# Attention on one core: the value products moved into fewer, longer runs between turns and scores

## The reference, cut to what matters

```
for blk in range(S // Q_BLOCK):                       # 16 blocks of 128 queries
    s = einsum("bhqd,bhkd->bhqk", q[block], k[:q1])   # scores against all earlier keys
    s = s + cum[q] - cum[k]                           # forget gates
    p = softmax(where(causal, s, -inf))
    outs.append(einsum("bhqk,bhkd->bhqd", p, v[:q1])) # value products
```

## Time and profile before

| | |
|---|---|
| median of 3 runs | 2429.84 us (2429.21 to 2431.21) |
| the profiled execution's own time | 2430.31 us |
| its span, first to last instruction | 2428.5 us |
| TensorE clock granted, mean | 0.995 |
| PE busy | 2377.7 us, 98% |
| DVE busy | 1355.0 us, 56% |
| ACT busy | 1121.2 us, 46% |
| the attention in the span | about 704 to 1534 us |

### The profile page before, as it was taken

One profiled execution on the slowest core, in us unless ns is written; L12 is line 12 of the kernel. 1 busy time (PEld: TensorE's weight loads), 2 busy tenths in 40 slices (PEclk: granted clock), 3 DMA queues, 4 the chain that ended last, 5 costly groups with the idle time before them and its releaser, 6 DMA issues. The chain is left out here.

```text
span 2428.5 us, 36529 instructions
## 1 busy us (share of the span) xinstructions
PE 2377.7 (98%) x13441; PEld 2046.7 (84%) x13441; DVE 1355.0 (56%) x2766; ACT 1121.2 (46%) x2036; POOL 616.3 (25%) x717
## 2 busy tenths in 40 slices
PE   8999999999999999999999999989999999999998
PEld 7888889999887888888888888877888888887787
DVE  4232112111014888888888888836544566667633
ACT  2131111101115888888888888832014465657300
POOL 0000000000001455554555554525430000000343
PEclk9999999999999999999999999999999999999999
DMA  6525444232126454566544566266533453447672
GB/s 200 141 75 140 114 121 122 105 122 104 65 90 150 98 117 110 119 138 136 119 117 110 121 137 138 89 204 207 180 122 98 141 160 126 136 136 248 222 256 82
DMA packets 221258, 328.78 MB, mean 135 GB/s; under 512 B 17420, under 2 KB 144716, under 8 KB 215260
## 3 DMA queue, kind: packets, MB, share of 16 engines
q1 hardware_dynamic: 220568, 325.91, 47.2%
q0 software_dynamic: 512, 0.53, 0.1%
HBM read 199.89 MB, written 126.48 MB: 134 GB/s over the span
## 5 line engine op out<-in xcount | busy, mean ns | idle before, releaser
L926 DVE TENSOR_TENSOR at_pl<-at_tps,at_ph 128x512 fp32r<-128x512 f32 (+3 forms) x640 | 371.1, 605 | 16.0 <-ACT at_ph L849 16.0
L849 ACT ACTIVATE at_ph<-at_tps 128x512 fp32r<-128x512 f32 (+3 forms) x640 | 319.1, 537 | 125.7 <-PE at_tps L763 117.7
L324 ACT ACTIVATE pa_stg<-pa_ps 128x512 fp32r<-128x512 f32 (+1 forms) x128 | 76.5, 598 | 635.9 <-PE pa_ps L252 635.9
L763 PE MATMUL at_tps<-ident,at_probs 128*128 128x128 f32 x2176 | 340.6, 274 | 8.5 <-DVE at_pl L926 7.2
L783 PE MATMUL at_ops<-at_ph,at_val 128*128 128x256 f32 (+1 forms) x1152 | 315.5, 296 | 0.2 <-DVE at_pl L926 0.2
L839 ACT ACTIVATE at_probs<-at_probs,at_least 128x128 f32<-128x128 f32 (+15 forms) x256 | 308.0, 1203 | 0.1
L252 PE MATMUL pa_ps<-pa_xh,pa_wh 128*128 128x512 f32 x768 | 300.3, 391 | 3.4 <-DVE pa_wl L377 3.4
L252 PE MATMUL pa_ps<-pa_xh,pa_wl 128*128 128x512 f32 x768 | 299.4, 390 | 0.0
L252 PE MATMUL pa_ps<-pa_xl,pa_wh 128*128 128x512 f32 x768 | 299.3, 390 | 0.0
L783 PE MATMUL at_ops<-at_pl,at_val 128*128 128x256 f32 (+1 forms) x1152 | 294.9, 282 | 0.0
L749 PE MATMUL at_sps<-at_k,at_q 128*128 128x512 f32 (+3 forms) x640 | 277.8, 434 | 10.3 <-DVE at_probs L918 7.8
(11 more groups left out here) (184 smaller groups left out, 4624.8 us busy)
## 6 DMA issues: line engine op xcount, KB each, us to landing
at_q<-q_halves SPq DMA_DIRECT2D x45, 512.0 KB
at_k<-k_halves SPq DMA_DIRECT2D x45, 512.0 KB
q_halves<-pa_stg SPq DMA_DIRECT2D x32, 512.0 KB, 3.8
k_halves<-pa_stg SPq DMA_DIRECT2D x32, 512.0 KB, 3.7
v_halves<-pa_stg SPq DMA_DIRECT2D x32, 512.0 KB, 2.8
y_gated<-re_work SPq DMA_DIRECT2D x32, 512.0 KB, 3.1
at_val<-v_halves SPq DMA_DIRECT2D x15, 1024.0 KB, 17.3
pa_wst<-in_attn_w_in SPq DMA_DIRECT2D x14, 1024.0 KB, 7.1
```

What stands on the lines that cost most here:

```text
L324: nc.scalar.activation(out, source(kind, s), func, scale=scale).then_inc(evac_h, 1)
L763: mm = nc.tensor.transpose(tps[c % TB][:, k, :], probs[s % ROWS][:, t0:t0 + P], ident[:, :])
L849: nc.scalar.activation(ph[g % 2][:, j * PB:j * PB + n, i % 2 * P:(i % 2 + 1) * P], tps[c % TB][:, 0:n, :], ACT.Copy).then_inc(high_out, 1)
L926: nc.vector.tensor_tensor(pl[g % 2][at], tps[c % TB][:, 0:n, :], raw(ph[g % 2][at]), ALU.subtract)\
```

## The change: where value products stand in a step

The change is in `step` of the tensor program. It makes a list `slots` of the places behind which value products may stand: the parts that have a turn next, and the last part. Of these it keeps every second one, counted so that the last stays in; it drops those ahead of j = 3, but keeps the last one if nothing is left. The step's value products are then divided evenly over the slots. How many key tiles a step multiplies, and every other engine's program, stay as they are.

```diff
                 order = alternate(scores_now, turns, -1)
+                slots = [j for j in range(parts) if j + 1 == parts or order[j + 1][0]]
+                slots = slots[(len(slots) + 1) % 2::2]
+                slots = [j for j in slots if j >= SKIP] or slots[-1:]
                 for j in range(parts):
                     if order and order[j][0]:
                         turn(t_it, t_s, order[j][1])
                     elif order:
                         score(it, s, order[j][1])
-                    if weighing:
-                        k0, k1_ = (lo + (hi - lo) * max(j + d - SKIP, 0) // max(parts - SKIP, 1) for d in range(2))
-                        if j + 1 == parts:
-                            k1_ = hi
+                    if weighing and j in slots:
+                        k0, k1_ = (lo + (hi - lo) * (slots.index(j) + d) // len(slots) for d in range(2))
                         if k1_ > k0:
                             weigh(w_it, w_g, k0, k1_)
```

## The result

The changed kernel takes 2440.61 us (median of 6 runs, 2438.09 to 2442.19) against 2430.68 for the kernel before on the same chips: a ratio of 1.0039, 95% interval 1.003 to 1.0049, or 9.9 us more. The forecast was slower, 2447 us, with a range of 2430 to 2456. The sign and the mechanism were right; 9.9 us were measured of the 17 that the sum gave. Of all executions in this study one, the profiled one of the kernel with less work in block 1, took 5990 us and is left out.

A forecast was written before the change was run, and what follows sets the result against it. PE was taken to bound blocks 0 to 4, DVE blocks 8 to 15. Lateness behind last scores and in block 15 summed to 1.11 us a head, 17 us taken on 2430: 2447 us, range 2430 to 2456.

The forecast's parts named there:

- the sum: Lateness after blocks 9 and 11 to 14, and in block 15: 1.11 us a head, 17.8 us over 16 heads, taken as 17.
- the mechanism: Blocks 8 to 14: products behind a step's last score, which a take pins, delay the next block's second score, by 0.02 to 0.28.
- What bounds blocks 8 to 15: DVE takes and subtracts back to back (24.37 of 25.13 us busy in blocks 8 to 14); PE, though seemingly busy, waits.
- the signs that were named: DVE waits at second takes and block 15's third; blocks 8 to 14 grow 0.7 to 0.8 us, block 15 some 0.35.
- the term for the arrival: From PE's end of a score to the take waiting for it: 0.29 us, used in every line from block 9 to 15.
- The extra time of a score that has waited: A score that waited runs slower: 0.57 us full, 0.28 for 128 columns, 0.38 and 0.47 interpolated for 256 and 384.
- the lower end: If a score that waited cost no more than any other, the sum would be 0.66 us a head, 11 us.
- Late by 0.35, if the second score came just in time: Block 15, second to third take: PE needs 1.63 us with three key tiles ahead of the third turn, DVE 1.28.
- The cost of 0: Blocks 0 to 2: products move behind the fourth turn, PE's sum decides and stays the same; neither cost nor gain.
- Hidden: Rival: DVE's few tenths in hand absorb PE's lateness in blocks 9 to 15; within 0.2%, 2430 to 2435; chance 0.17.
- Faster: Rival: PE bounds throughout, and scores following turns at once remove half its 33 us of waits: 2414 us; chance 0.08.
- Much slower: Rival: DVE has nothing in hand, every key tile moved in blocks 8 to 15 counts whole: 65 us, 2495; chance 0.05.

The follow-up runs named there:

- blocks 12 to 14 alone: New rule for product portions in blocks 12, 13 and 14 only, old rule elsewhere, against the kernel before: 2438.93 us, ratio 1.0038.
- the kernel with the early fourth turn: Kernel before, but in block 15 no products ahead of the fourth turn, two key tiles behind it, four at the end: 2429.58 us, ratio 0.9998.
- the combined kernel: Kernel before with block 15's fourth turn early, half of block 0's products ahead of its third turn, blocks 0 to 2's rest behind the fourth: 2426.51 us, 0.9983.

## Why the prediction was right, and what its sum got wrong

*What bounds blocks 8 to 15.* Right. VectorE is back to back there, PE waits, and taking 0.48 us of PE's work out of blocks 9, 11 and 13 gained nothing in any of them.

*The mechanism.* Right, and shown from two sides. The last score of a step is pinned by a take; what stands behind it delays the next block's scores. The same run ahead of that score costs nothing (ratio 1.0006), behind it 8 us (1.0038 with blocks 12 to 14 alone). For a run of 4 or 5 key tiles it is the place and not the length as such. Of the signs that were named, PE's waits moved from a first score to the last ones, and blocks 0 to 4 kept their time; but blocks 8 to 14 grew by 0.36 us and not by 0.7 to 0.8, and the takes that came late were the first ones, and not the second.

*The size.* The step that was off is the term for the arrival, "from PE's end of a score to a take that waits for it ... 0.29 us", as applied to second takes. It was read at a first take. After the change, first takes start 0.30 us behind their score's end (1260.00 to 1260.30), but second takes at most 0.21 (1260.91 to 1261.12), without waiting, and the third take of block 15, which does wait, 0.20. With the first takes as the ones that come late, the prediction's own terms give 0.08 at block 9, 0.09 at 12 (0.82 + 0.28 + 0.94 + 0.91 + 0.29 = 3.24 against 1253.43 - 1250.28 = 3.15), 0.18 at 13, 0 at 14, and with an arrival of 0.20 in block 15, 0.26. That is 0.61 us a head, where 0.61 was measured (0.04, 0.11, 0.15, 0.01, 0.29, and 0.01 here and there). That the two are equal is in part luck: the single blocks are off by up to 0.04 both ways, and the 0.20 is read from the very take whose delay it is to give. The extra time of a score that has waited, for which the lower end was worked out, was right: 0.27 to 0.28 us for 128 columns in the new trace too (1257.85 to 1258.12). So the 9.9 us lie near the lower end of 11, but not for that end's reason. The rule of the Trainium skill that was weighed there (TensorE: Matmul & The Clock Gate, What happens when you issue a matmul: weight loads are pulled ahead of matmuls in flight) does not help a score that waits: in the new trace it is again the weight load that is held, 88 times for 43.9 us, and the matmul behind it for 8.1 us.

*Block 15.* "Late by 0.35, if the second score came just in time" was the right form: alone it costs 0.00, behind blocks 12 to 14 it costs 0.29. What I had not seen is that the lead, once lost, is paid in any case: with the old order in block 15 it came out in blocks 0 to 3, so that the loss belongs to blocks 12 to 14. Of these, block 14's run takes the lead away even where block 13's is shorter.

*Blocks 0 to 2.* The cost of 0 was right, for a wrong reason. "PE is busy all the time" there, "PE's sum decides": it does not. PE's modelled ends cover its waits: the stretch shows 15.97 us busy of 15.97, with a wait of 0.62 us in front of block 0's third turn and the 0.36 in front of block 3's first product in it. Leaving work out of block 1 gained little or nothing and filling the wait of block 0 nothing, and only block 3 gave its 0.48 us back. The chain of waits as the runs show it: from block 15's fourth turn over ScalarE to the lows of block 2, for which the first product of block 3 waits. In the kernel before, ScalarE goes without a break from 1212.37, where it waited for that turn, to the lows' inputs of block 2:

```profile
1212.37 0.28 ACT L849 ACTIVATE at_ph<-at_tps 128x128 fp32r<-128x128 f32 x1 [0.45 <-PE at_tps L763]
1212.55 1.90 ACT L839 ACTIVATE at_probs<-at_probs,at_least 128x1920 f32<-128x1920 f32 x1
...
1215.23 1.85 ACT L849 ACTIVATE at_ph<-at_tps 128x512 fp32r<-128x512 f32 x4
1216.94 2.02 ACT L839 ACTIVATE at_probs<-at_probs,at_least 128x2048 f32<-128x2048 f32 x1
...
1218.93 1.97 ACT L849 ACTIVATE at_ph<-at_tps 128x512 fp32r<-128x512 f32 x4
...
1221.93 2.31 ACT L849 ACTIVATE at_ph<-at_tps 128x512 fp32r<-128x512 f32 x4
```

and VectorE's four lows of block 2 follow, 1222.57 to 1225.05, right up to the product at 1225.10 that is shown above with its wait of 0.36 us. Only from there to block 4 is PE the bound. That the second chain, PE's own from block 0's third turn, is nearly as long is shown by ScalarE's new wait in the kernel with the early fourth turn and by the combined kernel, which gains where each part alone does not; how the remaining 0.19 us a head in front of block 3 divides between ScalarE and VectorE was not tried.

*The rivals.* "Hidden" failed because the lateness at 12 and 13 is more than the lead; it is what blocks 8 to 11 and block 15 do alone. "Faster" failed as VectorE has nothing to gain. "Much slower" failed by far: PE's lead covers most of the moved products.

## What to carry to other kernels

When two engines take turns, find the instruction that a buffer pins to the other engine's progress, and put filler work ahead of it, where the engine would wait anyway, and behind it no more than the lead over the other engine covers. Ahead of it a run of 4 or 5 key tiles cost nothing here; behind it the length counts: with three key tiles in place of five in block 13, that block's 0.15 us fell to 0.01. A busy share of 100% from modelled ends does not show a bound: leave 0.5 us of work out of one stage at a time, and see which stage gives it back. A lead that is lost in one stage may be paid in a later one, so that judging a stage by its own time puts the loss in the wrong place.

## What the runs showed of the hardware that was not expected

Where VectorE waits for a score, it starts the take 0.29 to 0.30 us after PE is done with it if it is the first take of block 4, 13 or 14, and 0.20 us after if it is the third take of block 15. Second takes followed their scores by 0.21 us in blocks 13 and 14 without waiting, which gives a bound only. The cause of the difference wasn't tried.
